# Residual gate row: from one plain float32 product per half to two products of high and low parts

## The reference

```python
mod = jax.nn.silu(c) @ w_ada[layer] + b_ada[layer]
shift, scale, gate = jnp.split(mod, 3, axis=-1)
h = rmsnorm(x, norm_gain[layer]) * (1.0 + scale[:, None, :]) + shift[:, None, :]
proj = h @ w_in[layer]
...   # pooling branch y_a, sparse attention branch y_b
merged = jax.nn.sigmoid(g_a) * (y_a @ w_branch_a[layer]) + jax.nn.sigmoid(g_b) * (y_b @ w_branch_b[layer])
x = x + gate[:, None, :] * (merged @ w_out[layer])
```

## Time and profile before

| | us |
|---|---|
| median of 3 runs (lowest, highest) | 815.76 (815.57, 817.72) |
| the profiled execution's own time | 817.25 |
| its span, first to last instruction | 815.5 |
| PE busy in the span | 799.6 |
| DVE, ACT, POOL busy | 579.3, 351.9, 336.7 |

### The profile page before, as it was taken

One profiled execution on the slowest core, in us unless ns is written; L12 is line 12 of the kernel. 1 busy time (PEld: TensorE's weight loads), 2 busy tenths in 40 slices (PEclk: granted clock), 3 DMA queues, 4 the chain that ended last, 5 costly groups with the idle time before them and its releaser, 6 DMA issues.

```text
span 815.5 us, 12768 instructions
## 1 busy us (share of the span) xinstructions
PE 799.6 (98%) x4419; PEld 679.1 (83%) x4419; DVE 579.3 (71%) x1198; ACT 351.9 (43%) x644; POOL 336.7 (41%) x311
## 2 busy tenths in 40 slices
PE   7999999999999999999999999999999999999998
PEld 5988998887888888887878877789888897888987
DVE  6777588797888888888898616456667885772522
ACT  5664456663212222233241222687778883420200
POOL 1000524153535459851662212575888812540000
PEclk8899999999999999999999999999999999999999
DMA  9940110023242321230123323733433113753421
GB/s 341 386 127 1 53 52 27 1 59 103 103 123 78 104 77 30 87 116 27 52 78 103 104 85 106 234 141 110 131 106 114 40 42 134 253 168 122 135 97 58
DMA packets 59881, 87.87 MB, mean 108 GB/s; under 512 B 5514, under 2 KB 36526, under 8 KB 59823
## 3 DMA queue, kind: packets, MB, share of 16 engines
q1 hardware_dynamic: 48482, 65.07, 25.2%
q10 hardware_dynamic: 9420, 15.75, 5.2%
q0 software_dynamic: 1920, 6.29, 2.0%
HBM read 66.12 MB, written 20.97 MB: 107 GB/s over the span
## 4 chain that ended last, share of the span: by engine, by line
PE 88%; DVE 5%; ACT 2%; issue 2%; DVEq 1%; DMA 1%; POOLq 0%; ACTq 0%; POOL 0%
PE pp L724 21%; PE pp L726 21%; PE pp L725 21%; PE pp L1174 4%; PE pt L1149 3%; PE ps L965 3%; PE ps L964 3%; DVE score L2102 2%; PE pt L783 1%; PE ps L798 1%; DMA col_rows<-in_b_ada 1%; DVE prob L2260 1%; PE pt L1082 1%; DVE pT L2190 1%; PE ps L805 1%
## 5 line engine op out<-in xcount | busy, mean ns | idle before, releaser
L2127 DVE TENSOR_SCALAR_CACHE_REDUCE junk<-score,cand 128x384 uint8<-128x384 f32 (+1 forms) x186 | 168.6, 944 | 19.3 <-issue 13.3
L724 PE MATMUL pp<-hT_hi,w_hi 128*128 128x512 f32 x384 | 150.2, 391 | 0.0
L726 PE MATMUL pp<-hT_hi,w_lo 128*128 128x512 f32 x384 | 149.5, 389 | 0.0
L725 PE MATMUL pp<-hT_lo,w_hi 128*128 128x512 f32 x384 | 149.5, 389 | 0.0
L667 POOL TENSOR_TENSOR w_lo<-w_raw,w_hi 128x1024 fp32r<-128x1024 f32 x39 | 96.2, 2482 | 116.1 <-ACT w_hi L662 114.9
L724 PEld LDWEIGHTS pp<-hT_hi,w_hi 128*128 128x128 f32 x384 | 72.1, 188 | 16.1 <-issue 0.8
L726 PEld LDWEIGHTS pp<-hT_hi,w_lo 128*128 128x128 f32 x384 | 72.1, 188 | 15.0
L725 PEld LDWEIGHTS pp<-hT_lo,w_hi 128*128 128x128 f32 x384 | 72.1, 188 | 14.8
L2190 DVE TENSOR_TENSOR pT<-pt,pT 128x512 fp32r<-128x512 f32 (+3 forms) x96 | 50.5, 554 | 45.0 <-ACT pT L1577 41.7
L1461 ACT ACTIVATE stage<-pp 128x512 f32<-128x512 f32 x32 | 19.2, 599 | 126.6 <-PE pp L726 126.6
L662 ACT ACTIVATE w_hi<-w_raw 128x1024 fp32r<-128x1024 f32 x52 | 52.9, 1054 | 44.8 <-PE pp L726 40.9
(11 more groups left out here) (311 smaller groups left out, 1831.1 us busy)
## 6 DMA issues: line engine op xcount, KB each, us to landing
w_raw<-in_w_in SPq DMA_DIRECT2D x36, 512.0 KB, 3.6
sgb_spill<-stage ACTq DMA_DIRECT2D x16, 256.0 KB, 2.0
sga_spill<-stage ACTq DMA_DIRECT2D x16, 256.0 KB, 2.0
stage<-sga_spill SPq DMA_DIRECT2D x16, 256.0 KB, 3.1
ma_spill<-stage POOLq DMA_DIRECT2D x16, 256.0 KB, 2.8
gate_w<-in_w_ada SPq DMA_DIRECT2D x16, 256.0 KB, 2.8
w_raw<-in_w_out SPq DMA_DIRECT2D x8, 512.0 KB, 4.6
e_in<-sgb_spill SPq DMA_DIRECT2D x16, 256.0 KB, 3.1
```

What stands on the lines that cost most here:

```text
L724: nc.tensor.matmul(o, a_hi, b_hi, start=first, stop=False)
L725: nc.tensor.matmul(o, a_hi, b_lo, start=False, stop=False)
L726: return nc.tensor.matmul(o, a_lo, b_hi, start=False, stop=last)
L2127: v.tensor_scalar(junk[:, n % 2, 0:keys(b)], score[:, score_at(b):score_at(b + 1)], least, None, ALU.is_ge, ALU.add, accum_out=cnt[:, n:n ...
```

## The change

The matrix of ones in fp32r replaces the one in float32: it is written by ACT into the first 128 columns of `wg_hi`, whose weights of the pooling branch are no longer needed. In its step 63 (`i == HEADS - 1`) ACT writes this matrix and then the high part `gate_hi` of all 1024 columns of `gate_acc`. DVE writes the low part `gate_lo`, one half at a time into one buffer of 512 columns, at the ends of its steps 65 and 70 (`GATE_LOW`); the second write must wait until PE has read the first. PE then makes each half's row of two products, ones by high and ones by low, where one plain float32 product stood. The three tiles share the memory of `gate_w`.

```diff
+    GATE_LOW = {65: 0, 70: 1}
...
+                gate_hi, gate_lo = alloc(k, "gate_hi", [P, 2, HALF], F32R), alloc(k, "gate_lo", [P, HALF], F32R)
...
                 if i in GATE_ROWS:
                     g = GATE_ROWS[i]
-                    pe.wait_ge(gate_sum, g + 1)
-                    nc.tensor.matmul(pt_claim(("gate", g))[:], ones[:], gate_acc[:, g * HALF:(g + 1) * HALF],
-                                     start=True, stop=True).then_inc(pt_full, 1)
+                    pe.wait_ge(gate_hi_done, g + 1)
+                    pe.wait_ge(gate_lo_done, g + 1)
+                    o = pt_claim(("gate", g))
+                    nc.tensor.matmul(o[:], wg_hi[:, 0, :], gate_hi[:, g, :], start=True, stop=False)
+                    nc.tensor.matmul(o[:], wg_hi[:, 0, :], gate_lo[:], start=False, stop=True).then_inc(pt_full, 1)
...
+                if i == HEADS - 1:
+                    nc.scalar.activation(wg_hi[:, 0, :], ones[:], ACT.Copy)
+                    act.wait_ge(gate_sum, 2)
+                    act.wait_ge(gate_used, 2 * KD)
+                    nc.scalar.activation(gate_hi[:].rearrange("p g n -> p (g n)"), gate_acc[:],
+                                         ACT.Copy).then_inc(gate_hi_done, 2)
...
+                if i in GATE_LOW:
+                    g = GATE_LOW[i]
+                    dve.wait_ge(gate_hi_done, g + 1)
+                    if g:
+                        dve.wait_ge(pt_full, pt_at[("gate", 0)] + 1)
+                    v.tensor_tensor(gate_lo[:], gate_acc[:, g * HALF:(g + 1) * HALF], gate_hi[:, g, :].bitcast(F32),
+                                    ALU.subtract).then_inc(gate_lo_done, 1)
```

More of the change, by code:

```diff
@@ L390, in tenants_c @@
             alloc(s, "zone_s", [P, 8 * 256])
-            gate_w = alloc(s, "gate_w", [P, 3, HALF])
+            with ExitStack() as k:
+                gate_w = alloc(k, "gate_w", [P, 3, HALF])
+            with ExitStack() as k:
+                gate_hi, gate_lo = alloc(k, "gate_hi", [P, 2, HALF], F32R), alloc(k, "gate_lo", [P, HALF], F32R)
+            alloc(s, "zone_g", [P, 3 * HALF])
             alloc(s, "below_rel", [P, 64])
@@ L400, in tenants_c @@
             return (yT_hi, yT_lo, ua, win, z_silu, mixed, bias, a_out, e_in, stage, eq, (eqT0, eqT1), m_raw, junk,
-                    gate, gate_acc, gate_w, x_row, o_row)
+                    gate, gate_acc, gate_w, x_row, o_row, gate_hi, gate_lo)
         (shift_w, x_in, ada_acc, shift_b, kv_hi, kv_lo), ta, tc = zone(70.5, tenants_first, tenants_a, tenants_c)
@@ L405, in hybrid_layer @@
         (yT_hi, yT_lo, ua, win, z_silu, mixed, bias, a_out, e_in, stage, eq, eqT, m_raw, junk,
-         gate, gate_acc, gate_w, x_row, o_row) = tc
+         gate, gate_acc, gate_w, x_row, o_row, gate_hi, gate_lo) = tc
         q_row, z_row, q_stk, qT = att["q_row"], att["z_row"], att["q_stk"], att["qT"]
@@ L457, in hybrid_layer @@
         gate_sum, gate_used, gate_row_in = sem("gate_sum"), sem("gate_used"), sem("gate_row_in")
+        gate_hi_done, gate_lo_done = sem("gate_hi_done"), sem("gate_lo_done")
         gate_in = [sem(f"gate_in{i}") for i in range(3)]
```

## The result

The changed kernel takes 819.38 us in the median of 22 runs (817.26 to 823.49), and the kernel before 817.4 us in 22 runs beside them (815.47 to 821.06). The ratio is 1.0024, with a 95% interval of 1.0013 to 1.0035: 2 us slower, which lies within the 0.3% of the prediction. The forecast was 817.7 us in a range of 816.2 to 819.3, so the measured time is 1.7 above the forecast and 0.08 above the range. The profiled execution took 821.04 us with a span of 819.3.

What follows compares the result with a forecast made beforehand. PE was taken as the bound, busy 799.6 of 815.5 us. Terms -0.80 (products) + 0.45 (ACT) + 2.31 (wait) = +1.96 us gave 819.2 for the profiled execution and 817.7 us in the median, range 816.2 to 819.3.

Steps and rivals of the forecast that it cites:

- the last of the sum: Whole kernel: profiled execution would take 819.2 us; the median of runs lies 1.49 below it, so 817.7 us.
- The products: PE's two gate rows: two fp32r products at 0.46 us replace 0.86 each, 0.80 us less for both.
- ACT's copies: ACT ahead of the copy to oT: ones matrix and gate_hi make PE 0.45 us late, ends 0.2 and 0.8.
- The first gate_lo: DVE in step 65: subtraction of 0.68 us fits in 1.50 us of idle time and costs nothing.
- The round at gate row 1: PE waits for block 6's transposes, ACT's high part, DVE's low part, gate_lo: 2.07 plus 0.24, 2.31 us.
- what `gate_lo` does to DVE's merges: DVE behind the second gate_lo: second merge begins 0.3 us later but costs nothing, as PE is itself later.
- (a): Gate row 1: waits are hidden and PE's gain arrives, -0.35 us, 815.4 us, or 815.0; chance 0.06.
- (b): Behind the wait at gate row 1: PE's clock falls, 7 us lost, 824.7 us; chance 0.05.
- (c): Second gate_lo runs beside POOL and takes up to 2.88 us, adding 2.2 us: 819.9 us; chance 0.03.
- (d): Hand-over to ACT and DVE at 723.26 or output stage: delay is given back, about 816.5 us; chance 0.06.

Runs made afterwards that it cites:

- e4: Changed kernel with ACT copies in step 66 and both gate_lo halves in own memory, written in steps 67 and 68; 816.65 us, ratio 0.9995.
- e2: Changed kernel with the plain float32 product of each gate row put back, all new waits, copies and subtractions kept; 820.62 us, ratio 1.0046.
- e3: Kernel before plus only the two ACT copies in step 63, gate rows plain, no gate_lo; 817.89 us, ratio 1.0006.
- e5: Changed kernel with both gate_lo halves in own memory, written in steps 65 and 67, ACT copies left in step 63; 816.44 us, ratio 0.9992.
- e1: Changed kernel with DVE writing the second gate_lo in step 69 instead of 70; 817.45 us, ratio 1.0.
- e6: Changed kernel with the second gate_lo one place further back on DVE, behind the second merge; 822.71 us, ratio 1.0075.
- e9: Changed kernel plus 8 extra idle-filling products in the first 45 us; 818.28 us, ratio 1.0013.
- e10: Changed kernel with the second gate_lo behind the second merge, plus 8 extra products in the first 45 us; 821.42 us, ratio 1.0045.
- e11: Changed kernel plus 8 extra products in the first 45 us, run once more; 819.21 us, ratio 1.0014.
- e7: Kernel before plus 8 extra idle-filling products of 512 columns in the first 45 us; 815.79 us, ratio 0.9981.
- e8: Changed kernel with ACT copies in step 66, gate_lo halves early in own memory, plus 8 extra products in the first 45 us; 814.82 us, ratio 0.9971.
- e12: Changed kernel with ACT copies in step 66, gate_lo halves early in own memory, plus 8 extra products at the start, run again; 814.95 us, ratio 0.9968.

## Why the prediction was right or wrong

**The baseline was wrong, and by that the time.** The step that failed is the last of the sum: "The median of the runs is 1.49 below that execution: 817.7 us." The difference of +1.96 us is what was measured: 819.38 - 817.4 = 1.98. That it fits to 0.02 us has luck in it: one term was 0.19 too large and another of 0.2 was missing (both below), and the medians can't tell less than 0.9 us. But the 815.76 us were the median of three, and two of the three (815.57 and 815.76) lie where later only executions with the highest mean clocks lie. Of 22 the median is 817.4, 0.15 us above the profiled one of 817.25, and they lie within 815.47 and 821.06, not within 2 us as the three did. Had I kept the profiled execution as the base, the forecast would have been 819.2 instead of 817.7, against the measured 819.38. The range inherited the low base and ended at 819.3; it also took runs that differ by some tenths, where the executions of the changed kernel lie within 817.26 and 823.49. The page's row of PEclk and the windows of the earlier trace rows showed the cause ahead of the result: a stretch at half clock in the start, of which I asked only what it might cost at gate row 1, and not whether it lasts equally long in each execution. It doesn't: 14 us in the profile of before, 17 in that of the changed kernel, 7 in that of e4.

**The products.** Forecast 0.80 us of gain, measured 0.76 by e2 and 0.89 by e4.

**ACT's copies.** The mechanism was right, the size too large: 0.45 forecast, 0.26 by e3 and again by e5 against e4. The copy to `oT` came 0.42 us later and not 0.6 to 0.7, since the overlap of about 0.1 us that I took once stands at three borders: `gate_hi` starts 0.19 us behind the start of a copy that takes 0.31, for one. On the chain PE idles for 0.10 us and its transposes take 0.63 instead of the 0.44 of the transposes elsewhere: 0.29 us.

**The first gate_lo.** Forecast as free; it was in DVE's idle time, which went from 1.50 to 0.90 us:

```profile
675.05 0.68 DVE L2290 TENSOR_TENSOR gate_lo<-gate_acc,gate_hi 128x512 fp32r<-128x512 f32 x1
...
676.63 1.29 DVE L2204 TENSOR_TENSOR pT<-pt,pT 128x512 fp32r<-128x512 f32 x2 [0.90 <-ACT pT L1585]
```

**The round at gate row 1.** Forecast 2.07 us of wait and 0.24 of refill, measured 2.06 and 0.24 (0.47 against 0.23). By e1 it goes with the place of one DVE instruction, by e6 it grows with what is put in front.

**What was missing.** I costed what `gate_lo` does to DVE's merges at nothing. The chain has a pause of 0.22 us at 696.82. By the times, PE waits there for the buffer of a unit of branch B that DVE frees with the product of a merge (695.97 + 0.68 = 696.65). That merge is 0.2 us late against PE, and one merge earlier DVE and POOL come in another order than before:

```profile
693.60 1.29 POOL L1855 TENSOR_TENSOR mT_lo<-m_raw,mT_hi 128x512 fp32r<-128x512 f32 x1 [9.98 <-ACT mT_hi L1623]
...
693.76 1.68 DVE L2250 TENSOR_TENSOR m_raw<-m_raw,e_in 128x512 f32<-128x512 f32 x1 [0.45 <-issue]
...
695.97 0.68 DVE L2248 TENSOR_TENSOR m_raw<-pp,e_in 128x512 f32<-128x512 f32 x1
```

DVE's addition took 1.68 us where it takes 0.69 alone. The Trainium skill, SBUF — State Buffer (section "Who interferes with whom"), says that a VectorE instruction with two SBUF inputs contends with a GpSimd one that reads SBUF, and calls it an exclusive lock; the trace agrees, for the addition ends at 695.44, 0.55 us behind POOL's end at 694.89. The collision itself isn't new. In the kernel before DVE's addition starts ahead of POOL (690.02 in the earlier trace rows), and the collision falls on the subtraction behind it, without a pause of PE:

```profile
689.83 0.69 DVE L2236 TENSOR_TENSOR m_raw<-m_raw,e_in 128x512 f32<-128x512 f32 x1
690.44 1.78 DVE L2241 TENSOR_TENSOR mT_lo<-m_raw,mT_hi 128x512 fp32r<-128x512 f32 x1
...
692.15 0.68 DVE L2234 TENSOR_TENSOR m_raw<-pp,e_in 128x512 f32<-128x512 f32 x1
```

From the end of gate row 1 the last of these rows is 7.58 us away, its counterpart in the changed kernel 7.81. POOL comes first in the changed kernel, e1, e2, e6, e9, e10 and e11, thus where the second `gate_lo` stands among or just ahead of merges in steps 69 and 70, and DVE first in before, e3, e4, e5, e7, e8 and e12. What holds DVE for the 0.45 us ahead of the addition isn't shown.

The sum of the terms as measured, -0.80 for the products on the chain (0.76 by e2) + 0.26 + 2.30 + 0.2, is 1.96, against the distance's 1.91.

**The rivals.** (a) did not come: the changed kernel has the full wait, and what it would have been worth is e5, 0.63 us under before. (b), to which I gave 0.05, is shown for the wait of 3.44 us alone, at some 1.6 us and not 7. For the wait of 2.06 us it isn't shown: PEclk is 1.00 behind it in three profiles, and in the medians of changed and before nothing stands out, 1.98 against 1.91 by the distance. On the start of e7 something does (changed less e8 3.5 and less e12 4.3 us, where the distances say 2.7 and 2.8), but whether those falls lie behind the wait or in the start is open. (c) did not come at gate row 1, where `gate_lo` took 0.68 us with POOL idle; its mechanism showed 7 us later, on the addition of a merge, where a collision with POOL stood before the change too. (d) did not come: from the end of gate row 1 to the end of the span it is 815.5 - 684.57 = 130.93 us before and 819.3 - 688.16 = 131.14 changed, so nothing came back and the pause of 0.2 was added.

## What to carry to other kernels

Before an instruction of the bound engine is made cheaper by splitting its input on other engines, find the last event in front of each split in the queue of its engine; if that event is something the bound engine has just made, it will wait for a full round, here 2.3 us against a gain of 0.4. Read a profiled execution against several runs, and look whether the clock in the start differs between them, before subtracting one from the other: three executions were 1.6 us off. And compare two traces by the distance from a common instruction ahead of the change to the end, which here told 0.1 us where the medians of a dozen runs told no better than 1.

## What the runs showed of the hardware

PE's clock fell to the 1.2 GHz level behind an idle time of 3.44 us that followed four short transposes, and stayed there through dense products from 687.9 to 691.3 us in e6; that cost 1.6 us. In e10 it fell at the same place. Behind the idle time of 2.06 us in the changed kernel, e9 and e11 it stayed at 1.00 in the executions that were profiled. Eight further products of 512 columns in the first 45 us, which compute nothing that is used, made the kernel before 2 us faster in the median and narrowed its runs from 6 us to 2.5. With them ten of twelve executions had a mean clock of 0.998 or more; of the 24 beside them none had more than 0.997.
